# A scan's bypassed operand moved to a PSUM bank, two transpose banks for three, and values matmuls placed between the transposes

## What is computed

```
def _sb_block(q, k, v, q_pos, k_pos, bias):
    z = jnp.einsum('bqhd,bkhd->bhqk', q, k) * (SB_HEAD_DIM ** -0.5) + bias[None, :, None, None]
    vis = k_pos[None, :] < q_pos[:, None]
    log_keep = jnp.where(vis, jax.nn.log_sigmoid(-z), 0.0)
    after = lax.cumsum(log_keep, axis=3, reverse=True) - log_keep
    a = jnp.where(vis, jnp.exp(jax.nn.log_sigmoid(z) + after), 0.0)
    return jnp.einsum('bhqk,bkhd->bqhd', a, v)
```

## Time and profile before

| | us |
|---|---|
| median of 3 runs (2844.94 to 2848.82) | 2846.69 |
| the profiled execution | 2847.92 |
| its span in the trace | 2846.1 |
| TensorE busy in the span (87%) | 2470.6 |
| VectorE busy (43%) | 1235.7 |
| ScalarE busy (32%) | 908.0 |
| GpSimd busy (33%) | 935.8 |

### The profile page before, as it was taken

One profiled execution on the slowest core, in us unless ns is written; L12 is line 12 of the kernel. 1 busy time (PEld: TensorE's weight loads), 2 busy tenths in 40 slices (PEclk: granted clock), 3 DMA queues, 4 the chain that ended last, 5 costly groups with the idle time before them and its releaser, 6 DMA issues. The chain is left out here.

```text
span 2846.1 us, 37750 instructions
## 1 busy us (share of the span) xinstructions
PE 2470.6 (87%) x14209; PEld 1568.9 (55%) x14209; DVE 1235.7 (43%) x1625; ACT 908.0 (32%) x1746; POOL 935.8 (33%) x479
## 2 busy tenths in 40 slices
PE   5999899999499997899999874888888877886998
PEld 3555444444244443788888772555556555553443
DVE  1111056675300000555555424878687853441333
ACT  2222021232100001222223203878787852221110
POOL 2333010011000000544444203867786870003554
PEclk9999999999799998899999956999999988997999
DMA  5223211211222321111111018031220008994332
GB/s 149 98 92 100 45 38 46 62 32 45 54 57 42 80 90 49 39 30 44 31 43 42 18 36 195 16 65 34 57 48 16 16 14 304 324 318 166 130 130 84
DMA packets 161790, 233.32 MB, mean 82 GB/s; under 512 B 16496, under 2 KB 95361, under 8 KB 156568
## 3 DMA queue, kind: packets, MB, share of 16 engines
q1 hardware_dynamic: 161688, 231.93, 27.4%
HBM read 162.97 MB, written 68.91 MB: 81 GB/s over the span
## 5 line engine op out<-in xcount | busy, mean ns | idle before, releaser
L1599 POOL TENSOR_TENSOR f_a<-f_a,f_keep 128x144 f32<-128x144 f32 (+15 forms) x128 | 445.4, 3498 | 154.0 <-DVE f_keep L1545 154.0
L1545 DVE TENSOR_TENSOR_SCAN f_keep<-f_keep 128x144 f32<-128x144 f32 (+15 forms) x128 | 439.3, 3437 | 129.0 <-ACT f_a L1517 129.0
L614 PE MATMUL ps<-hT,wa 128*128 128x512 f32 (+1 forms) x960 | 353.6, 531 | 39.7 <-DMA wa<-w_in 39.0
L448 PE MATMUL ps<-hT,wc 128*128 128x512 f32 (+1 forms) x960 | 354.1, 531 | 12.3 <-DMA wc<-w_in 12.3
L614 PEld LDWEIGHTS ps<-hT,wa 128*128 128x128 f32 x960 | 168.3, 191 | 225.0 <-issue 225.0
L448 PEld LDWEIGHTS ps<-hT,wc 128*128 128x128 f32 x960 | 168.6, 191 | 197.0 <-issue 197.0
L1464 PE MATMUL ps<-con,f_a 128*128 128x128 f32 x1216 | 185.0, 294 | 70.6 <-POOL f_a L1599 69.3
L2012 PE MATMUL ps<-m_w,m_mT 128*128 128x512 f32 x544 | 238.0, 596 | 0.0
L322 PE MATMUL ps<-wt,hT_now 128*128 128x512 f32 x544 | 237.9, 595 | 0.0
L1443 PE MATMUL ps<-f_k,f_q 64*128 64x344 f32 (+19 forms) x832 | 186.2, 526 | 35.1 <-DMA f_k<-chan 34.6
L1464 PEld LDWEIGHTS ps<-con,f_a 128*128 128x128 f32 x1216 | 141.2, 149 | 109.8 <-POOL f_a L1599 87.3
(11 more groups left out here) (277 smaller groups left out, 3335.4 us busy)
## 6 DMA issues: line engine op xcount, KB each, us to landing
j_kp<-cache_k SPq DMA_DIRECT2D x128, 256.0 KB, 3.9
j_v<-cache_v SPq DMA_DIRECT2D x128, 256.0 KB, 4.7
chan<-y SPq DMA_DIRECT2D x12, 1088.0 KB, 6.0
chan<-ya SPq DMA_DIRECT2D x12, 1088.0 KB, 11.5
d_ld<-chan SPq DMA_DIRECT2D x16, 768.0 KB, 5.0
h_rows<-hg SPq DMA_DIRECT2D x17, 512.0 KB, 5.0
m_hh<-h_rows SPq DMA_DIRECT2D x17, 512.0 KB, 3.3
f_k<-chan SPq DMA_DIRECT2D x16, 516.0 KB, 14.5
```

What stands on the lines that cost most here:

```text
L448: m = pe.matmul(ps[:, ci, 0:n], wc[k][:, c, :], hT[:, c, c0:c0 + n], start=(c == 0), stop=(c == KC - 1))
L614: m = pe.matmul(ps[:, ci, 0:n], wc[k][:, c, :], hT[:, c, c0:c0 + n], start=(c == 0), stop=(c == KC - 1))
L1545: dve.tensor_tensor_scan(x, x, x, 1.0, ALU.mult, ALU.bypass).then_inc(scanned, 1)
L1599: pool.tensor_tensor(w, w, keep[i % KEEPS][:, L - n + 1:L + 1], ALU.mult).then_inc(weighed, 1)
```

## The change

Four things change, all in `prompt_attention`.

1. The second, bypassed operand of the scan is no longer `keep`: it is one column of PSUM bank 6 (set to 1.0 once), read with stride 0 over the whole length.
2. That bank is taken from the transposes, which now go to two banks (4 and 5): turn number n waits for the copy of number n - 2.
3. The values matmuls of a row pair no longer stand in one burst at the beginning of an even iteration. In an odd iteration values(m, g - 1) follows turn(j, g) for g = 1, 2, ...; only the last group is left at the beginning of the next even iteration, behind scores(i, 0).
4. The unused copies on VectorE and their counters are taken out.

```
+TURNS = 2
...
-    Z_BANK, T_BANK, O_BANK = 0, 4, 7
+    Z_BANK, T_BANK, IDLE_BANK, O_BANK = 0, 4, 6, 7
...
-                if n >= 3:
-                    if by_vector[n - 3]:
-                        pe.wait_ge(out_dve, START + vector_to[n - 2])
-                    else:
-                        pe.wait_ge(out_act, START + scalar_to[n - 2])
+                if n >= TURNS:
+                    pe.wait_ge(out_act, START + n - TURNS + 1)
...
-                    m = pe.transpose(ps[:, T_BANK + n % 3, j * P:(j + 1) * P], a[i % RING][:, c + b * P:c + (b + 1) * P], p.ident)
+                    m = pe.transpose(ps[:, T_BANK + n % TURNS, j * P:(j + 1) * P], a[i % RING][:, c + b * P:c + (b + 1) * P], p.ident)
...
-                pe.wait_ge(out_dve, START + vector_to[done])
-                pe.wait_ge(out_act, START + scalar_to[done])
+                pe.wait_ge(out_act, START + done)
...
                     if x == 0 and j >= 1 and j % 2 == 0:
-                        for g in range(groups[j - 1]):
-                            values(j // 2 - 1, g)
+                        values(j // 2 - 1, groups[j - 1] - 1)
                     for g in range(2 * x, min(2 * x + 2, ng)):
                         turn(j, g)
+                        if j % 2 and g:
+                            values(j // 2, g - 1)
...
-                act.activation(at[i % 2][:, 512 * g:512 * g + nb], ps[:, T_BANK + n % 3, 0:nb], ACT.Copy).then_inc(out_act, 1)
+                act.activation(at[i % 2][:, 512 * g:512 * g + nb], ps[:, T_BANK + n % TURNS, 0:nb], ACT.Copy).then_inc(out_act, 1)
...
-                dve.tensor_tensor_scan(x, x, x, 1.0, ALU.mult, ALU.bypass).then_inc(scanned, 1)
+                dve.tensor_tensor_scan(x, x, ps[:, IDLE_BANK, 0:1].broadcast_to([P, n]), 1.0, ALU.mult, ALU.bypass).then_inc(scanned, 1)
...
+            x = dve.memset(ps[:, IDLE_BANK, 0:1], 1.0)
             x.then_inc(filled_v, 1)
...
             for i in range(N + LAG + 1):
                 j = i - LAG
-                ng = groups[j] if 0 <= j < N else 0
-                for g in range(0, min(2, ng)):
-                    out(j, g)
                 if 1 <= i <= N:
                     scan(i - 1)
                 if j >= 1 and j % 2 == 0:
                     gate(j // 2 - 1)
-                for g in range(2, ng):
-                    out(j, g)
```

More of the change, by code:

```diff
@@ L1346, in prompt_attention @@
     groups_to = np.cumsum([0] + groups).tolist()
-    by_vector = [False for n in range(groups_to[-1])]
-    vector_to = np.cumsum([0] + by_vector).tolist()
-    scalar_to = [n - v for n, v in enumerate(vector_to)]
     values_to = np.cumsum([0] + groups[1::2]).tolist()
@@ L1356, in prompt_attention @@
     mask_filled = p.sem("diagonal_filled")
-    turned, out_act, out_dve, av_done = p.sem("A_turned"), p.sem("AT_by_scalar"), p.sem("AT_by_vector"), p.sem("av_done")
+    turned, out_act, av_done = p.sem("A_turned"), p.sem("AT_by_scalar"), p.sem("av_done")
     gated, stored = p.sem("po_gated"), [p.sem(f"po{b}_stored") for b in range(2)]
     filled_v, filled_p, ready = p.sem("pa_filled"), p.sem("pa_padded"), p.sem("pa_bias_ready")
-    Z_BANK, T_BANK, O_BANK = 0, 4, 7
+    Z_BANK, T_BANK, IDLE_BANK, O_BANK = 0, 4, 6, 7
     with ExitStack() as st:
@@ L1520, in out @@
                 n = groups_to[i] + g
-                if by_vector[n]:
-                    return
                 nb = min(4, row_of(i) + 2 - 4 * g) * P
                 act.wait_ge(turned, START + n + 1)
-                act.activation(at[i % 2][:, 512 * g:512 * g + nb], ps[:, T_BANK + n % 3, 0:nb], ACT.Copy).then_inc(out_act, 1)
+                act.activation(at[i % 2][:, 512 * g:512 * g + nb], ps[:, T_BANK + n % TURNS, 0:nb], ACT.Copy).then_inc(out_act, 1)
             act.wait_ge(ready, START + 2)
```

## The result

The changed kernel takes 2899.3 us in the median (2894.0 to 2903.3, 4 runs) against 2845.8 for the kernel before (four runs; the 2846.7 of the prediction is the median of three of them), a ratio of 1.0185 with a 95% interval of 1.0163 to 1.0208: 1.85% slower. The forecast was 2882, slower, in a range of 2830 to 2915. The profiled execution took 2902.8 us (span 2901.0), 54.9 more than the one before. The rest of the span did not change: 2242.5 us outside the attention, for 2243.7.

A forecast was written before the change was run, and what follows sets the result against it. The prediction took VectorE's scan and GpSimd's multiplication, running in turn, to bound the attention stage. Its terms, -64 + 75 + 14 + 19 - 10 = +34 us, gave 2882 us, range 2830 to 2915.

The forecast's parts named there:

- 20 for the two banks: Transposes in prompt attention: two banks instead of three alone cost some 20 us.
- third rival: Prompt attention: scan still excludes multiplication beside the same TensorE waits; +35 to +45 us, 2882 to 2892; chance 0.07.
- The port: Scan operand in PSUM: scan and multiplication overlap, TensorE's waits for the multiplication go; -64 us, bounds -69 to -55.
- The 75: Values matmuls, odd iterations: values(.,0) waits for a ScalarE copy behind two sigmoids; +75 us, bounds 65 to 80.
- the 19: Two transpose banks and the second piece: values(.,2) waits plus late ScalarE; +19 us together, bounds 0 to 38.
- the 6 for values(.,2): Rows 11 to 13: values(.,2) waits 0.7 us for a copy behind gates(i,1); 6 us in all.
- ScalarE's lateness: After even iterations ScalarE is late by 0.2 to 0.8 us, adding to the next odd wait; 13 us.
- the burst's waits: TensorE's waits for copies in the old values burst, 16.4 us, mostly go; -10 us, bounds -16 to 0.
- changes between kinds of work: TensorE: values groups between transposes add 0.17 us on each side; +14 us, bounds 0 to 24.
- low ends: Lower bounds of all the forecast's terms for the attention stage, said to give -26 us together.
- fourth rival: TensorE's clock drops after idling; a tenth of its work at 1.2 GHz gives +50 us, 2930; chance 0.07.
- first rival: Faster, 2807 or 2787: waits go if 2.6 us of TensorE work covers them or copy precedes sigmoids; chance 0.16.

The follow-up runs named there:

- e1: The changed kernel with the values matmuls in one burst again, scan operand in PSUM and two transpose banks kept: 2802.2 us, ratio 0.9847.
- e4: The kernel before with two transpose banks for three (unused copies also taken out), scan from SBUF, values in one burst: 2847.5 us, ratio 1.0010.
- e5: The changed kernel with values still spread between transposes, but one iteration later, where their copies are done: 2806.9 us, ratio 0.9873.
- e3: The kernel before with only the values matmuls in their new places, three banks, scan from SBUF: 2912.5 us, ratio 1.0233.
- e2: The changed kernel with the scan's bypassed operand back in SBUF, spread values and two banks kept: 2904.5 us, ratio 1.0213.
- e10: e2 plus eight transposes of a constant into the idle bank before values(j//2,0), odd iterations, rows 3 to 13: 2887.0 us, ratio 1.0141.
- e9: e5 with two groups of values and then two of transposes, so kinds of work change half as often: 2788.3 us, ratio 0.9793.
- e8: The changed kernel with ScalarE's copies out(j,0), out(j,1) ahead of the sigmoids gates(i,0): 2852.5 us, ratio 1.0026.
- e7: The changed kernel with values split by head, each iteration running one head's values of the item before in one burst: 2885.7 us, ratio 1.0149.

## Why the prediction held, and where it was off

**What bounds before: right.** Scan and multiplication took turns, and the PSUM operand ends that: mean 2451 ns where about 2460 was forecast, and 2140 for the multiplication where 2140 was; a scan of 1936 elements takes 4.19 us, forecast 4.2. A stride-0 operand in PSUM costs a scan nothing that shows. The gain alone: e1 came to 2802 us, where the prediction's terms that apply to it, 2847 - 64 + 20 for the two banks, make 2803. That fit is partly luck, since the sum has only waits in it: from e4 to e1 TensorE's busy time at a granted clock of 0.50 also falls, from 47.1 to 12.4 us.

**Where the gain went: right.** The values' waits for copies of the same iteration take more than it. e1, e5 and e3 show that this step makes the loss; e2 shows the third rival's point, that the total hardly depends on the port while the waits are there (the trace of after excludes that rival itself).

**The size: 54.9 us in the profiled executions where the sum had 34.** Term by term, in TensorE's own time of the stage, which grew by 658.5 - 602.4 = 56.1 us:
- The port: -64 forecast, -69.3 measured (the waits of the earlier trace rows are all gone; the 5 us kept for the last rows were not needed).
- Waits for copies: 75 + 19 - 10 = 84 forecast; measured (90.0 + 23.4) against (16.4 + 1.3) before, 95.7. The 75 are 75.0 in the trace, but that agreement is partly luck: row 14 waits 1.90 us for 0.5 forecast, and rows 4, 5 and 9 to 13 wait less than forecast. Of the 19, the 6 for values(.,2) are 6.1; ScalarE's lateness, put at 13, is 22.1 at the transposes. Of the burst's waits 7.6 us went, for 10 forecast.
- TensorE's busy time: 14 us forecast for changes between kinds of work, at most 24; measured 535.8 - 505.8 = 30.0. e5 against e1, both with two banks and with the same little time at the lower clock, has 23.7 for the changes alone. The other 6 stay open. At the values line slow stretches come on top (181.6 for 168.6 in e5), at the transposes there are fewer of them than before; over the stage they come to the same, as shown below. So the two mis-sized terms are ScalarE's lateness and the changes.

Two slips in the working changed little: the low ends add up to -20 and not -26, and 0.7 us in rows 11 to 13 of four pairs are 8.4 us and not 6.

**"I expect none", of the fourth rival, was wrong of the clock and right in the sum, by luck.** From one row, transposes at full speed after 1.90 us of idle time, I concluded that waits of up to 2 us leave the clock alone. The trace of before has the opposite too: 8 transposes after a wait of 1.66 us take 1.77 us at a granted clock of 0.50, where they take 1.09 at full clock. After has 14 such stretches, each beside a wait at the values line of 1.25 to 1.92 us; behind some, as at 1848.11, lies another wait close by, behind others, as at 1896.08, none.

```profile
1959.72 1.77 PE L1464 MATMUL ps<-con,f_a 128*128 128x128 f32 x8 [1.66 <-POOL f_a L1599]
```

```profile
1896.08 1.98 PE L1474 MATMUL ps<-f_at,f_v 128*64 128x128 f32 x16 [1.90 <-ACT f_at L1518]
```

Most waits of this length are followed by full speed; what tells them apart stays open. e10 prices the slow stretches at some 17 to 21 us. But they are no part of the 54.9: before had as many, behind its waits for the multiplication. The stretches of the stage at a granted clock of 0.50, added up, are 14 in before and 15 in after, with one at the start of the stage in each (their length, then TensorE's busy time in them; first before, then after):

```profile
sum 66.13, PE 56.43; mean PE 4.03
```

```profile
sum 66.78, PE 56.82; mean PE 3.79
```

The waits that the PSUM operand removed had slow stretches behind them, and the waits that the new places brought have as many: two terms that the prediction did not have, and that cancel.

**The first rival's condition was wrong in one half.** A wait for older copies does remove the loss (e5, e9); useful work between scores and values was not tried. Moving the copy ahead of the sigmoids doesn't (e8: 2852.5 and not 2807): it puts the wait for the transposes in front of the sigmoids, and the scores behind them wait instead.

## What to carry to other kernels

A matmul stream that runs in order is filled with work whose inputs were finished an iteration ago; work placed "between" the steps that produce its inputs waits for the whole queue of the engine that makes them, and everything behind it waits too. Before a step is moved, write down both engines' orders side by side and count what lies between the wait and its release on each. Two changes that meet in one stage are to be timed apart: here the PSUM operand is worth 1.6% beside a burst of values and nothing that can be told beside the new places, which lose 2.3% alone.

## What the runs showed of the hardware that was not expected

- The values matmuls of two heads, which alternate and write different halves of the partitions (0 to 63 and 64 to 127), run side by side. With both heads in turn, 68 instructions take 3.93 us (e1's last burst); with one head alone, 34 instructions take 3.93 us (e7's last burst). Splitting them by head doubled the line's time, 148.2 to 293.9 us.

```profile
2294.31 3.93 PE L1474 MATMUL ps<-f_at,f_v 128*64 128x128 f32 x68
```

```profile
2373.90 3.93 PE L1473 MATMUL ps<-f_at,f_v 128*64 128x128 f32 x34
```

- Transposes whose result nobody reads, put where TensorE waits anyway, made a kernel 17 us faster (e2 to e10): the work behind them then ran at 2.4 GHz (granted clock 0.98 in the stage, for 0.95).
- Waits of TensorE between 1.25 and 1.92 us, 14 of the 71 at the values line in after, were followed by work at a granted clock of 0.50.
